# Two chained models on one core: the modulation of the first model's layers, summed by another engine in another place

## What is computed

```python
def layer(x, cx, c_silu, cctx_silu, norm_w, ada_w, ada_b, w_in, w_out, ...):
    mod = c_silu @ ada_w + ada_b            # ada_w: 1024 x 3072
    mod_c = cctx_silu @ ada_w + ada_b
    shift, scale, gate = jnp.split(mod, 3, axis=-1)
    shift_c, scale_c, gate_c = jnp.split(mod_c, 3, axis=-1)
    hx = rmsnorm(x, norm_w) * (1 + scale[:, None, :]) + shift[:, None, :]
    hc = rmsnorm(cx, norm_w) * (1 + scale_c) + shift_c
    ...
    x = x + gate[:, None, :] * (ux @ w_out)
```

## Time and profile before

| | |
|---|---|
| time, median of 3 runs | 1830.4 us (1830.12 to 1832.49) |
| profiled execution, its own span | 1831.0 us |
| PE busy | 1796.1 us, 98% |
| DVE busy | 1267.7 us, 69% |
| ACT busy | 1083.3 us, 59% |
| moved by DMA | 285.24 MB, mean 156 GB/s |

### The profile page before, as it was taken

One profiled execution on the slowest core, in us unless ns is written; L12 is line 12 of the kernel. 1 busy time (PEld: TensorE's weight loads), 2 busy tenths in 40 slices (PEclk: granted clock), 3 DMA queues, 4 the chain that ended last, 5 costly groups with the idle time before them and its releaser, 6 DMA issues.

```text
span 1831.0 us, 34169 instructions
## 1 busy us (share of the span) xinstructions
PE 1796.1 (98%) x13208; PEld 1561.0 (85%) x13208; DVE 1267.7 (69%) x2284; ACT 1083.3 (59%) x1907; POOL 54.5 (3%) x56
## 2 busy tenths in 40 slices
PE   7999999999999999999999999999999999999998
PEld 5878878879888988889888988889888889998887
DVE  6663354478726677776688787767776679788765
ACT  5372274385737477764556667746774556667762
POOL 0000000004000000001000000000000000000001
PEclk9999999999999999999999999999999999999999
DMA  9232242242234314555542455545555642355553
GB/s 351 106 117 87 97 163 109 93 149 96 87 114 145 116 71 175 188 188 194 188 151 95 163 182 190 196 174 198 183 187 180 233 161 105 127 184 184 187 186 132
DMA packets 42506, 285.24 MB, mean 156 GB/s; under 512 B 4928, under 2 KB 6336, under 8 KB 9360
## 3 DMA queue, kind: packets, MB, share of 16 engines
q1 hardware_dynamic: 40832, 278.24, 42.2%
q0 software_dynamic: 1552, 5.29, 0.9%
HBM read 282.46 MB, written 1.05 MB: 155 GB/s over the span
## 4 chain that ended last, share of the span: by engine, by line
PE 91%; ACT 3%; DVE 3%; issue 1%; DMA 1%; SPq 0%; POOL 0%; DVEq 0%; ACTq 0%
PE bank L2357 26%; PE bank L2351 14%; PE bank L2353 13%; PE bank L2352 13%; PE bank L2358 13%; PE bank L2648 3%; PE bank L2596 3%; PE bank L2548 2%; ACT work L1111 1%; PE bank L2456 1%; PE bank L2533 1%; DMA token_major<-weights 1%; DVE panels_lo L1518 1%; ACT token_major L1087 1%; PE bank L2576 0%
## 5 line engine op out<-in xcount | busy, mean ns | idle before, releaser
L2357 PE MATMUL bank<-acts,panels_hi 128*128 128x512 f32 x2032 | 710.6, 396 | 0.6 <-DVE panels_lo L1518 0.6
L1518 DVE TENSOR_TENSOR panels_lo<-raw_panels,panels_hi 128x1024 fp32r<-128x1024 f32 x468 | 573.3, 1242 | 184.9 <-ACT panels_hi L958 183.1
L958 ACT ACTIVATE panels_hi<-raw_panels 128x1024 fp32r<-128x1024 f32 x468 | 484.2, 1054 | 248.3 <-PE bank L2353 152.9
L2358 PE MATMUL bank<-acts,panels_lo 128*128 128x256 f32 x2032 | 565.1, 278 | 0.0
L2357 PEld LDWEIGHTS bank<-acts,panels_hi 128*128 128x128 f32 x2032 | 381.2, 188 | 91.7 <-DVE panels_lo L1518 1.4
L2358 PEld LDWEIGHTS bank<-acts,panels_lo 128*128 128x128 f32 x2032 | 382.1, 188 | 0.2
L2351 PE MATMUL bank<-acts,panels_hi 128*128 128x256 f32 (+1 forms) x1120 | 351.4, 314 | 1.1 <-DVE xT L1597 0.4
L2353 PE MATMUL bank<-acts,panels_lo 128*128 128x256 f32 (+1 forms) x1120 | 346.0, 309 | 0.0
L2352 PE MATMUL bank<-acts,panels_hi 128*128 128x256 f32 (+1 forms) x1120 | 346.0, 309 | 0.0
L2351 PEld LDWEIGHTS bank<-acts,panels_hi 128*128 128x128 f32 x1120 | 213.7, 191 | 18.4 <-issue 4.6
L2353 PEld LDWEIGHTS bank<-acts,panels_lo 128*128 128x128 f32 x1120 | 213.8, 191 | 10.9
(11 more groups left out here) (299 smaller groups left out, 1842.3 us busy)
## 6 DMA issues: line engine op xcount, KB each, us to landing
raw_panels<-weights SPq DMA_DIRECT2D x252, 1024.0 KB, 4.8
token_major<-weights SPq DMA_DIRECT2D x4, 1024.0 KB, 9.3
near_bias<-rpb POOLq DMA_DIRECT2D x12, 256.0 KB, 3.7
xT<-xin SPq DMA_DIRECT2D x4, 512.0 KB, 5.6
gates<-weights SPq DMA_DIRECT2D x2, 1024.0 KB, 10.1
near_bias<-weights SPq DMA_DIRECT2D x4, 512.0 KB, 7.3
token_major<-weights SPq DMA_DIRECT2D x2, 512.0 KB, 12.8
token_major<-rpb POOLq DMA_DIRECT2D x4, 256.0 KB, 3.4
```

What stands on the lines that cost most here:

```text
L958: act.activation(slot_hi(n, a, b), raw_of(n, a, b), ACT.Copy).then_inc(hi_ready, 1)
L1518: dve.tensor_tensor(slot_lo(n, a, b), raw_of(n, a, b), slot_hi(n, a, b).bitcast(F32), ALU.subtract).then_inc(lo_ready, 1)
L2357: pe.matmul(bank.rearrange("p (c t) -> p c t", c=2), whi_, with_rest(xhi_), start=start, stop=False, skip_group_check=True)
L2358: return pe.matmul(bank[:, 0:T], wlo_, xhi_, start=False, stop=stop, skip_group_check=True)
```

## The change

The sixteen panels leave the attentions, the weight stream, PE and ACT. Their products are formed by DVE with `tensor_tensor_reduce`. The weights of the gate of layer 0 and of all of layer 1 are stored on the host transposed, as 32 tiles of 128 output features by 1024 inputs (512 KB each, `MOD_TILES`). The rows c and c_ctx are loaded broadcast to all 128 partitions (1 MB) and go through SiLU on ACT. For each tile DVE multiplies it by a row and accumulates over the 1024 elements, once with c and once with c_ctx: 64 sums in all, the bias being the start value and the accumulator landing in the column of `mod` where it is needed. The products, which nobody reads, go to PSUM banks 4-5 and 6-7 in turn.

The sums come in three phases: 32 during qkvB, woutA and gateB of layer 0 (gate of layer 0, shift and scale's first tiles), 16 during qkvC and woutB of layer 0, and 16 during qkvB of layer 1. The table `MOD_AT` says after which piece of DVE's work how many are done. In the B phases two weight tiles are held at a time, in the C phase one. SP issues each tile's load between its panel loads, and waits before it for the sum that frees the buffer. New waits: in attention B, PE waits for all sums of the phase ahead of the last gate quarter (its bank is one of theirs); in gateC of layer 0, PE waits for all 48 sums ahead of its first turn, and ACT ahead of its first gate; the first output step of woutA waits for the gate's sums (layer 0) or for all of the phase (layer 1).

Attention itself: output banks 6 and 7 in turn now in layer 0 too. Of the next gate's panels, two halves are rounded and split in layer 0's attention, at steps 5 and 6 (before: those of one panel at one place and those of the panel after the last ada panel at another, four halves in all in A).

```diff
+MOD_PHASES = {("B", 0): (0, 16), ("C", 0): (16, 24), ("B", 1): (24, 32)}
+MOD_AT = {("B", 0): {"near0": (0, 3), "panel1": (3, 6), "panel2": (6, 8), "near2": (8, 11), "panel3": (11, 14), "panel4": (14, 17),
+                     "panel5": (17, 20), "out0": (20, 22), "out1": (22, 24), "out2": (24, 26), "out3": (26, 28),
+                     "gate0": (28, 30), "gate1": (30, 32)},
+          ("C", 0): {"panel1": (0, 2), "turned1": (2, 4), "panel2": (4, 6), "turned2": (6, 8), "out0": (8, 10), "out1": (10, 12),
+                     "out2": (12, 14), "out3": (14, 16)},
+          ("B", 1): {"near0": (0, 1), "panel1": (1, 3), "panel2": (3, 5), "near2": (5, 8), "panel3": (8, 10), "panel4": (10, 13),
+                     "panel5": (13, 16)}}
...
     def second_bank(blk, st):
-        return blk == 1 and st.layer == 1
+        return blk == 1
...
     def late_bank(m, l):
-        return banks[7 if l else 6]
+        return banks[7]
...
+        def mod_load(m, i):
+            first = MOD_PHASES[m, 0][0] if i < 24 else 24
+            held = 2 if m == "B" else 1
+            if i - first >= held:
+                sp.wait_ge(mod_sum, 2 * (i - held + 1))
+            sp.dma_start(mod_weights(m, i), modw[i]).then_inc(mod_landed(m, i)[0], 16)
...
+        for (m, l), counts in (("B", 0), (1, 2, 2, 2, 1, 3, 2, 1)), (("B", 1), (0, 1, 3, 1, 1)), (("C", 0), (0, 2, 3, 2)):
...
             freed_panel(before)
             sp.dma_start(raw_of(n, 0, PAN), weights[n]).then_inc(loaded[n % 2], 16)
+            for m, i in mod_loads.get(before, ()):
+                mod_load(m, i)
...
-                for r, slot in enumerate(ADA_SLOTS[mixer] if st.panels and blk == 1 else ()):
-                    n, row = st.at["panels"] + r, ADA_ROW[mixer] + r
-                    if i == slot + 1:
...
-                        act.activation(cmpw[:, 0:PW], banks[7][:, 0:PW], ACT.Copy).then_inc(row_out, 1)
...
-                if blk == 1 and 3 <= i + sooner < 5:
-                    round_half(ONE["gate" + mixer, st.layer].at["panels"] + 3, i + sooner - 3)
...
+                if blk == 1 and 5 <= i < 7:
+                    round_half(ONE["gate" + mixer, st.layer].at["panels"] + 3, i - 5)
...
+                        if j == 0 and (m, l) == ("C", 0):
+                            act.wait_ge(mod_sum, 2 * MOD_PHASES["C", 0][1])
...
+        def mod_sums(m, l, a, b):
+            for x in range(a, b):
+                i, v = MOD_PHASES[m, l][0] + x // 2, x % 2
+                layer, tile = MOD_TILES[i]
...
+                dve.wait_ge(*mod_landed(m, i))
...
+                if x >= 2:
+                    dve.wait_ge(mod_sum, 2 * MOD_PHASES[m, l][0] + x - 1)
+                dve.tensor_tensor_reduce(mod_products(x), mod_weights(m, i), c_rows(m)[:, v * D:(v + 1) * D], 1.0, add,
+                                         ALU.mult, ALU.add, to).then_inc(mod_sum, 1)
...
                 if late and i == 1:
+                    if mixer == "B":
+                        pe.wait_ge(mod_sum, 2 * MOD_PHASES["B", st.layer][1])
...
-                    if i == slot:
...
-                        ada_panel(st.at["panels"] + r, banks[7])
...
+                            if (m, l) == ("C", 0):
+                                pe.wait_ge(mod_sum, 2 * MOD_PHASES["C", 0][1])
```

More of the change, by code:

```diff
@@ L123, in attn @@
     def attn(m):
-        ada = ADA_IN[m][2] if ctx else 0
-        return Stage("attn" + m, l, panels=ada, ticks=ada,
+        return Stage("attn" + m, l,
                      units=24 if ctx else 16, groups=12 if ctx else 8, pairs=8 if ctx else 4)
@@ L203 @@
 PANEL_TICK, STEP_TICK = tick_tables()
-ADA_SET = {s.at["panels"] + r for s in ONE.values() if s.name.startswith(("ada", "attn")) for r in range(s.panels)}
+ADA_SET = {s.at["panels"] + r for s in ONE.values() if s.name == "ada" for r in range(s.panels)}
 NSA_G = TWO["nsa_g"].at["panels"]
@@ L1737, in attention @@
                     m.then_inc(omul, 1)
-                if blk == 1 and 4 <= i + sooner < 6:
-                    split_half(ONE["gate" + mixer, st.layer].at["panels"] + 3, i + sooner - 4)
-                for r, slot in enumerate(ADA_SLOTS[mixer] if st.panels and blk == 1 else ()):
-                    if 0 <= i + sooner - slot - 5 < 2:
-                        split_half(st.at["panels"] + r + 2, i + sooner - slot - 5)
+                if blk == 1 and 6 <= i < 8:
+                    split_half(ONE["gate" + mixer, st.layer].at["panels"] + 3, i - 6)
                 j = i - 1
@@ L2006, in rotate, with sums_at @@
                     dve.sem_inc(roped if j == 2 else q_roped, 1)
+            def sums_at(m, place, tile=None):
+                a, b = MOD_AT.get((m, l), {}).get(place, (0, 0))
+                if tile is not None:
+                    a, b = (a + tile, a + tile + 1) if a + tile < b else (0, 0)
+                if b > a:
+                    mod_sums(m, l, a, b)
             def qkv(m):
```

134 lines of the change are left out of this document (73 added, 61 removed).

## The result

| | median | runs | against the kernel before, same chip |
|---|---|---|---|
| before | 1830.5 us | 4, 1830.1 to 1832.5 | |
| after | 1845.2 us | 4, 1842.7 to 1848.0 | ratio 1.0078, 95% interval 1.0065 to 1.0090 |

The change makes the kernel slower by 0.78%, 14.6 us by the medians. That is the side and the likeliest case of the forecast, and 1845.2 lies inside the range, 0.8 us from its upper end; but the forecast stood at +5.1, so the size is nearly three times as large as forecast.

A forecast was written before the change was run, and what follows sets the result against it. PE was taken to bound the kernel, busy nearly throughout. From 1831.0 us, −12.4 + 12.6 + 1.9 + 0.4 + 2.6 = +5.1 gave 1836.1, less 0.6: 1835.5 us; range 1820 to 1846.

The forecast's parts named there:

- Attentions: Layer 0's attentions shrink without the panels, limited by ACT: −5.1 in A, −4.3 in B, −3.0 in C, together −12.4 us.
- gateA: Layer 0: rounding and splitting of a panel now falls between the turns, +0.4 us, ends 0 and 1.2.
- gateB: Layer 0: four sums behind the gates end at 239.0, after PE's last gate quarter wants to begin at 237.2: +1.9 us.
- The second bank: Two output banks in layer 0's attention: taken as nothing; spares a wait where DVE is late, and could not cost.
- The price of a sum: One DVE sum over 1024 elements with two fp32 SBUF operands: near 1.15 us from start to start.
- half-rate rival: A DVE sum with both operands from SBUF takes 2.3 us: kernel at 1861.9 us; chance 0.08.
- The load of a tile: A 512 KB weight tile lands in 3.2 to 3.4 us.
- qkvC and woutB: Layer 0: eight tiles through one buffer delay PE's first turn of gateC by +12.6 us; lower end +7.
- woutA of layer 1: Three sums ahead of the first output step make PE wait for its bank: +2.6 us, ends 0.7 and 3.5.
- The clock: No term in the sum; a clock that falls after a long wait was only part of the range's upper 10 us.
- The buffer cycle alone: DVE catches up on other work while tiles land; woutB costs only +7: 1829.9 us, no change; chance 0.20.
- Faster: Attentions shrink by all of 20.5 us and woutB costs +7: −8.6, 1821.8 us; chance 0.25.

The follow-up runs named there:

- kept_busy_3: Same kernel as `kept_busy_2`, run again beside a control without dummy products: 1846.7 us, ratio 1.0073 to the kernel before.
- sums_early: The change with the same 64 sums placed earlier in all phases, the last C-phase tile's products written in place: 1823.1 us, ratio 0.9954 to the kernel before.
- all_out: The change with all 64 sums, tile loads, rows of c and their SiLU left out: 1821.6 us, ratio 0.9944 to the kernel before.
- kept_busy: The change with 9 and 13 dummy products before PE's two woutB waits, C-phase products in one bank pair: 1847.2 us, ratio 1.0084 to the kernel before.
- kept_busy_2: `kept_busy` with 13 and 18 dummy products in place of 9 and 13: 1849.2 us, ratio 1.0092 to the kernel before.
- c_phase_out: The change with the C phase's 16 sums and 8 tile loads left out: 1829.0 us, ratio 0.9984 to the kernel before.

## Why the prediction was right, and where it was off

**Side and mechanism: right.** The three places where PE would wait were named. The profile shows the releasers of two, and the times of the sums show that of the third. Leaving out or moving the sums of the C phase, and moving those of the two B phases together, took the loss away. Term by term:

- *Attentions* (−12.4). Measured: −6.0 in A (forecast −5.1), −4.7 in B (−4.3). For C the stretch from the turn to the last values, 62.6 us before (342.29 to 404.85), is 60.1 in `kept_busy_3` and 60.7 in `sums_early`: −1.9 to −2.4 (−3.0), the clock apart. Together 12.6 to 13.1. The cap of 5.1 in A was wrong: PE's small waits there fell too, from 2.3 to 1.8 us; the other 0.4 is not explained. That ACT's step limits is borne out by PE's waits for it.
- *gateA* (+0.4): +1.1. The scores start that much later; the split takes nearly its upper end.
- *gateB* (+1.9; the prediction's own numbers, 239.0 − 237.2, give 1.8): 2.3.
- *The second bank* (0, "could not cost"): 0 in the time, but not for that reason. It took PE 3.8 us more of narrow spreads and saved it 3.4 us of waits.
- *The price of a sum* (1.15): 1.20. Here the prediction's own sum was made wrong: 0.61 + 512 × (1.24 − 0.07)/1024 is 1.20. Sixteen sums at 0.05 are 0.8 us of what the C phase was short of. The half-rate rival fell: the sums, both operands in SBUF and fp32, take 1.28 to 1.29 each and begin 1.20 apart where they follow each other. By what the Trainium skill says of the scalar-tensor-tensor shape ("Vector Engine (DVE) Microarchitecture Reference", section "7. Points that are easy to get wrong") it would have been about 2.3; the form that ran here is shown as a custom DVE instruction, so that sentence is neither borne out nor refuted for its own shape.
- *The load of a tile* (3.2 to 3.4): 3.6.
- *qkvC and woutB* (+12.6): 14.7 ahead of the turn. From the end of the first tile to the end of the eighth the layout had 44.9 us (309.9, which is 307.6 and a tile of 2.3, to 354.8), the trace 46.7 (303.4 to 350.2, the reads of the accumulators): a dearer sum and a slower landing in the seven steps between, partly hidden by DVE's other work. The order of events was as laid out, first output step behind the fourth tile, then the turn. The two waits were forecast at 3 to 4 and some 9 us and were 5.0 and 7.0; the slow clock behind the first, which the layout did not have, shortened the second.
- *woutA of layer 1* (+2.6): 2.98.
- *The clock* (no term). **This is the step that failed.** I allowed for "a clock that falls after a long wait" in the upper end of the range only. It is about 1.5 us at the turn of the change (2.3 where it stayed low for longer), and by the runs with and without the B phases' waits about 3 more behind these. It was to be had from the trace of before: there, too, PE's clock stood at 0.72 from 660 to 664 us, right behind a wait of 1.7 us in attention C of layer 1.

```profile
660.79 0.46 PE L2548 MATMUL bank<-consts_sb,work 64*128 64x64 f32 x8 [1.68 <-ACT token_major L1087]
```

```profile
660.00:664.00 4.00, 3.21 (x37) 2.81 (x38) 2.90 (x13) 3.66 (x9) 0.00 (x0) 0.72 0.73 262
```

The size: 5.1 forecast, 14.6 measured. On top of the forecast the terms above account for 2.1 in the C phase, 1.5 for the clock at the turn, 1.5 for gateA, gateB and woutA together, less 0.5 for the attentions, which makes 9.7, and with about 3 for the clock in the B phases, 12 to 13. The last two us stay open: 0.8 of them lie between attention A and the last values of attention B, where the change falls behind `all_out` by more than its wait, and the interval of the ratio is itself 4.6 us wide. That the range still held the result owes something to luck: its upper 10 us were meant for a landing or two more or a clock that falls, and what filled them was the clock and several smaller terms that all fell on the same side.

**The rivals.** "The buffer cycle alone" fell: PE waited for a step behind a landing, as said against it. "Faster" fell with both its halves: PE got back 12.6 to 13.1 us in the attentions and not 20.5, and the C phase cost 14.7 and not 7. That the kernel with the sums placed early takes 1822.7 to 1823.1 us, near this rival's 1821.8, is chance: it gets there with the smaller gain and sums that cost nothing. I had taken the placement as given, as a prediction must, but wrote that DVE has no freedom in it. The profile of the kernel before showed nine idle us ahead of the split that precedes the first sum:

```profile
305.32 2.36 DVE L1518 TENSOR_TENSOR panels_lo<-raw_panels,panels_hi 128x1024 fp32r<-128x1024 f32 x2 [8.94 <-ACT panels_hi L958]
```

That freedom, together with the new place of the last products, decides the sign.

## What to carry to other kernels

Work moved to an engine with idle time is free only if its pieces stand where the idle time is and none stands between a producer and the engine that sets the pace: the same 64 sums cost 24 us as first placed and nothing measurable when placed early, with the last tile's products out of PE's way. With one buffer, count the cycle of landing plus use from its first start to its deadline. Here it was enough to start it a panel earlier and to free PE of the last tile; a second buffer in the C phase was not tried. Price a wait of the engine that sets the pace with the slow clock behind it, except where a further wait follows whose end another engine sets.

## What the runs showed of the hardware

- PE's granted clock fell to half in or behind each of the eight waits of 4.7 to 8.3 us in woutB and ahead of gateC, and stayed there for the first 3 to 5 us of work. It fell behind one of 2.3 to 3.0 us in nine of sixteen cases (and at both waits of `kept_busy`), and behind the one of 1.7 us in attention C of layer 1 in nine of the thirteen profiles, that of the kernel before among them. With dummy products up to 0.65 us before the end of the wait it stayed at full in both waits of `kept_busy_2` and `kept_busy_3`.
- Stretches of about 3.4 us at half clock also come where PE was not waiting, at other places in each profile (432 and 1507 us in the change, 924 in `c_phase_out`, 1480 in `all_out`). Each costs some 1.7 us, an estimate from its length, and nothing here tells what sets their place.
- A DVE sum over two SBUF operands, right behind the one before, takes 1.20 us for 1024 elements from start to start; made to wait for the end of the one before, 1.50. With the products in SBUF instead of PSUM the first of these is 1.21 (337.26 to 338.47 in `sums_early`); for the second no run shows it.
